# Two transformer blocks on one core: a later slot for the last pair of heads, reordered small work in block 2, and the first input in smaller parts

## The reference

```python
for l in range(DEPTH):                       # block 2
    x = x + 0.5 * swiglu_2(rms_norm_2(x, norm_ffn1[l]), w_gate, w_up, w_down)
    x = x + hybrid_mixer(rms_norm_2(x, norm_mix[l]), w_in[l], ...)
    x = x + 0.5 * swiglu_2(rms_norm_2(x, norm_ffn2[l]), ...)
...
def compress(k, pos, w1, w2):                # keys (CK) and values (CV) of the compressed part
    blocks = k[:, :, cidx, :] + pos
    flat = blocks.reshape(B, G, n_cmp, CMP_LEN * Dh)
    return jax.nn.gelu(flat @ w1) @ w2
kc, vc = compress(k_cmp, ...), compress(v_cmp, ...)
p_c = masked_softmax(einsum(q, kc) * scale, valid_c)
o_cmp = einsum(p_c, vc)
```

## Time and profile before

| what | value |
|---|---|
| median of 3 runs | 2076.1 us (2075.55 to 2076.2) |
| the profiled execution: its time / its span | 2075.85 us / 2074.1 us |
| PE busy | 2048.1 us, 99% |
| POOL busy | 1579.3 us, 76% |
| ACT busy | 1083.4 us, 52% |
| DVE busy | 795.9 us, 38% |
| PE's share of the chain that ended last | 97% |

### The profile page before, as it was taken

One profiled execution on the slowest core, in us unless ns is written; L12 is line 12 of the kernel. 1 busy time (PEld: TensorE's weight loads), 2 busy tenths in 40 slices (PEclk: granted clock), 3 DMA queues, 4 the chain that ended last, 5 costly groups with the idle time before them and its releaser, 6 DMA issues.

```text
span 2074.1 us, 35496 instructions
## 1 busy us (share of the span) xinstructions
PE 2048.1 (99%) x12396; PEld 1769.1 (85%) x12396; DVE 795.9 (38%) x1788; ACT 1083.4 (52%) x1875; POOL 1579.3 (76%) x668
## 2 busy tenths in 40 slices
PE   8999999999999999999999999999999999999998
PEld 7888998888888898888888888788888889878886
DVE  3223744222322374422242237632233225663223
ACT  5445544444544553544454458654455445755443
POOL 7888746888888875688878886478887887546886
PEclk9999999999999999999999999999999999999999
DMA  7555534555555553455555554445555555454553
GB/s 248 191 185 183 183 113 124 191 190 187 179 186 189 176 183 113 132 190 187 190 175 190 182 191 138 166 162 190 187 189 179 185 183 183 139 184 156 186 191 112
DMA packets 100852, 362.33 MB, mean 175 GB/s; under 512 B 11808, under 2 KB 12448, under 8 KB 100640
## 3 DMA queue, kind: packets, MB, share of 16 engines
q1 hardware_dynamic: 100336, 359.97, 52.7%
q10 hardware_dynamic: 432, 1.22, 0.2%
HBM read 360.10 MB, written 1.05 MB: 174 GB/s over the span
## 4 chain that ended last, share of the span: by engine, by line
PE 97%; DVE 1%; ACT 1%; DMA 1%; issue 0%; ACTq 0%; SPq 0%; DVEq 0%; POOLq 0%
PE twin L591 31%; PE twin L595 20%; PE twin L653 9%; PE twin L655 9%; PE twin L654 9%; PE twin L593 5%; PE twin L594 4%; PE twin L710 1%; PE twin L637 1%; PE twin L767 1%; PE twin L638 1%; PE twin L639 1%; PE twin L773 1%; PE twin L784 1%; PE twin L840 0%; PE twin L1102 0%
## 5 line engine op out<-in xcount | busy, mean ns | idle before, releaser
L561 POOL TENSOR_TENSOR wlo<-raw,whi 128x1024 fp32r<-128x1024 f32 x664 | 1579.1, 2407 | 479.2 <-ACT whi L1260 478.9
L1260 ACT CAST whi<-raw 128x1024 fp32r<-128x1024 f32 x664 | 677.3, 1051 | 73.1 <-PE twin L595 35.6
L595 PE MATMUL twin<-turned,wlo 128*128 128x256 f32 x1952 | 549.7, 282 | 0.0
L591 PE MATMUL twin<-turned,whi 128*128 128x512 f32 x1344 | 480.3, 399 | 1.2 <-DVE turned L1640 1.2
L591 PE MATMUL twin<-early,whi 128*128 128x512 f32 x1344 | 480.0, 398 | 0.5
L595 PE MATMUL twin<-early,wlo 128*128 128x256 f32 x1536 | 431.2, 281 | 0.0
L1700 DVE TENSOR_TENSOR twin<-twin,mix 128x512 f32<-128x512 f32 x168 | 117.5, 699 | 758.0 <-ACT mix L1319 758.0
L595 PEld LDWEIGHTS twin<-turned,wlo 128*128 128x128 f32 x1952 | 371.0, 190 | 3.3
L1319 ACT COPY mix<-twin 128x512 f32<-128x512 f32 x168 | 98.5, 586 | 439.0 <-PE twin L595 439.0
L591 PEld LDWEIGHTS twin<-turned,whi 128*128 128x128 f32 x1344 | 253.1, 188 | 63.7 <-issue 1.6
L591 PEld LDWEIGHTS twin<-early,whi 128*128 128x128 f32 x1344 | 252.4, 188 | 64.2 <-issue 2.0
(11 more groups left out here) (285 smaller groups left out, 2092.6 us busy)
## 6 DMA issues: line engine op xcount, KB each, us to landing
raw<-in_w_dram SPq DMA_DIRECT2D x680, 512.0 KB, 3.3
con<-in_con_dram ACTq DMA_DIRECT2D x1, 1113.5 KB, 7.6
x<-in_x_dram SPq DMA_DIRECT2D x2, 512.0 KB, 6.5
out_dram<-xs SPq DMA_DIRECT2D x4, 256.0 KB, 2.8
mix<-in_last_gain_dram SPq DMA_DIRECT2D x1, 512.0 KB, 4.4
par<-in_par_dram SPq DMA_DIRECT2D x2, 208.0 KB, 4.0
par<-in_par_dram SPq DMA_DIRECT2D x2, 154.0 KB, 3.2
con<-in_con_dram ACTq DMA_DIRECT2D x1, 64.0 KB, 4.4
```

The source lines that it names most:

```text
L561: nc.gpsimd.tensor_tensor(wlo[:, place, :], raw[:, place, :], whi[:, place, :].bitcast(F32), ALU.subtract).then_inc(split_done, 1)
L591: pe.matmul(out, hi, both.rearrange("p c n -> p (c n)"), start=start and k == 0, stop=False, skip_group_check=True)
L595: mm = pe.matmul(out[:, 0:SEQ], lo, both[:, 0, :], start=False, stop=stop and k == KD - 1, skip_group_check=True)
L1260: nc.scalar.copy(whi[:, place, :], raw[:, place, :]).then_inc(hi_done, 1)
```

## The change

Four things are changed.

1. Block 2, in both layers: pair 11 is scored at slot 26 and no longer at 25; by the tables its turn moves from slot 27 to 28 and its weighting from 30 to 31. Pair 1's turn stands ahead of pair 3's scores at slot 12. On ACT, `hidden_exp(0)` stands behind slot 31's split and pair 11's exponentials. On DVE, the values' `hidden_kept(1)` stands ahead of the compressed maxima.
2. Start: the left half of x comes in two quarters with a semaphore each, and SyncE waits for slot 0 to land before it issues slot 1. TensorE turns the first quarter when it is there.
3. Start: slot 0's remainder is made by DVE; GpSimd begins with slot 1.
4. End: the two stores of the right half are issued by ACT, those of the left half by SyncE.

```diff
-SCORED = {..., 17: 8, 19: 9, 21: 10, 25: 11}
+SCORED = {..., 17: 8, 19: 9, 21: 10, 26: 11}
@@ SyncE, start
                         if n < 2:
-                            half = slice(n * 512, n * 512 + 512)
-                            sp.dma_start(x[:, :, half], x_d[:, :, half]).then_inc(s_x[n], 16)
+                            for j in range(2 - n):
+                                cols = slice(n * 512 + j * 256, 512 + n * 512 if n else 256 + j * 256)
+                                sp.dma_start(x[:, :, cols], x_d[:, :, cols]).then_inc(s_x[n + 2 * j], 16)
+                        if n == 0:
+                            sp.wait_ge(s_raw[0], 16)
@@ TensorE, x_turned
                 for j, out in zip((2 * half, 2 * half + 1), outs):
+                    if L.deep + w == 0 and j == 1:
+                        pe.wait_ge(s_x[2], 16)
@@ TensorE, block 2's mixer
                     if c in WEIGHED:
                         weighted(WEIGHED[c])
+                    if c in TURNED and TURNED[c] == 1:
+                        pair_turned(1)
                     if c in SCORED:
                         pair_scores(SCORED[c])
-                    if c in TURNED:
-                        p = TURNED[c]
-                        pe.wait_ge(ev("probs_ready"), L.l * PAIRS + (p + 1))
-                        turn_probs(L, p, m2("P", 2304)[:, p % 3 * 768:(p % 3 + 1) * 768])
+                    if c in TURNED and TURNED[c] != 1:
+                        pair_turned(TURNED[c])
@@ ScalarE, block 2's mixer
-                    if c - 1 == HID0_TURNED:
-                        hidden_exp(0)
                     ...                                  # split_hi(c + ahead), sums_kept
                     if c in SCORED:
                         pair_exps(SCORED[c])
+                    if c - 1 == HID0_TURNED:
+                        hidden_exp(0)
@@ VectorE, block 2's mixer
+                    if c == LAST[CV] + 1:
+                        hidden_kept(1)
                     if c - 1 == CMP_BACK:
                         ...                              # the compressed maxima
-                    if c in ENDED and ENDED[c] in (CK, CV):
-                        hidden_kept(int(ENDED[c] == CV))
+                    if c in ENDED and ENDED[c] == CK:
+                        hidden_kept(0)
@@ VectorE, start
+            dve.sem_inc(split_done, RING)
+            dve.wait_ge(hi_done, 1)
+            dve.tensor_tensor(wlo[:, 0, :], raw[:, 0, :], whi[:, 0, :].bitcast(F32), ALU.subtract).then_inc(split_done, 1)
@@ ScalarE, end (SyncE keeps the left half's two stores)
+            for at, T in enumerate(reversed(range(NT))):
+                act.wait_ge(ev("right_ready"), at + 1)
+                nc.scalar.dma_start(out_d[:, T, 512:D], xs[:, T, 512:D]).then_inc(s_out, 16)
```

More of the change, by code:

```diff
@@ L91 @@
 PAIRS = 12
-SCORED = {8: 0, 10: 1, 11: 2, 12: 3, 13: 4, 14: 5, 15: 6, 16: 7, 17: 8, 19: 9, 21: 10, 25: 11}
+SCORED = {8: 0, 10: 1, 11: 2, 12: 3, 13: 4, 14: 5, 15: 6, 16: 7, 17: 8, 19: 9, 21: 10, 26: 11}
 TURNED = {c + (5 if p == 10 else 2): p for c, p in SCORED.items()}
@@ L360, in m2 @@
             return mix[:, M2_[name]:M2_[name] + width]
-        s_x = [sem(f"x_loaded{half}") for half in range(2)]
+        s_x = [sem(f"x_loaded{part}") for part in range(3)]
         s_rest = sem("rest_of_con_loaded")
@@ L543, in _ @@
             for at, T in enumerate(reversed(range(NT))):
-                for half in range(2):
-                    cols = slice(half * 512, half * 512 + 512)
-                    sp.wait_ge(ev(("left_ready", "right_ready")[half]), at + 1)
-                    sp.dma_start(out_d[:, T, cols], xs[:, T, cols]).then_inc(s_out, 16)
+                sp.wait_ge(ev("left_ready"), at + 1)
+                sp.dma_start(out_d[:, T, 0:512], xs[:, T, 0:512]).then_inc(s_out, 16)
             sp.wait_ge(s_out, 2 * NT * 16)
@@ L561, in split_lo @@
                 nc.gpsimd.tensor_tensor(wlo[:, place, :], raw[:, place, :], whi[:, place, :].bitcast(F32), ALU.subtract).then_inc(split_done, 1)
-            pool.sem_inc(split_done, RING)
+            pool.wait_ge(split_done, 1 + RING)
             for L in layers:
                 mixer = MIX2 if L.blk else MIX1
-                with pool.Fori(0, FFN_SLOTS // RING) as i:
+                begun = L.deep == 0
+                if begun:
+                    for n in range(1, RING):
+                        split_lo(L, n)
+                with pool.Fori(0, FFN_SLOTS // RING - begun) as i:
                     for n in range(RING):
-                        split_lo(L, n, i)
+                        split_lo(L, n, i + begun)
                 for n in range(FFN_SLOTS, FFN_SLOTS + mixer):
@@ L1111, in value, with pair_turned @@
                     return vsw[:, c:c + HD]
+                def pair_turned(p):
+                    pe.wait_ge(ev("probs_ready"), L.l * PAIRS + (p + 1))
+                    turn_probs(L, p, m2("P", 2304)[:, p % 3 * 768:(p % 3 + 1) * 768])
                 def weighted(p):
```

## The result

The changed kernel takes 2082.53 us (median of 9 runs, 2080.57 to 2084.73), the kernel before 2075.9 us beside it (9 runs, 2075.06 to 2076.73). The ratio is 1.0032, 95% interval 1.0024 to 1.0040: slower by 6.6 us, where the prediction had 3.7. The profiled execution is the longest of the nine: 2084.73 us, with a span of 2082.9 us, 8.8 us over the span of before.

What follows compares the result with a forecast made beforehand. TensorE, busy for 99% of the span, was taken as the bound. Terms 2.2 + 2.5 - 0.9 - 0.1 = +3.7 us on 2075.85 gave 2079.55, or 2079.8 us against the runs' median; range 2076.2 to 2082.8 us.

Steps and rivals of the forecast that it cites:

- The mixer's chain: Block 2, slots 25 to 32: slot 31's split delays pair 11's exponentials, `compressed_keys` and slot 34's load; +2.2 and +2.5 us.
- Two signs: Waits expected in the changed trace: a short one at pair 11's turn for ScalarE, some 0.7 us at `compressed_values`.
- The forecast of 3.6 us for slot 34's load: Mixer, slots 30 to 32: time from the load's issue until taken up, against 3.9 us before and a 3.3 us median.
- the two layers cost 2.2 + 2.5: Block 2's mixers: `compressed_values` comes 2.2 us later in the first layer, slot 12 included; the second layer loses 2.5 us.
- The rival of late loads: Slot 34's load, which holds the compressed softmax, takes 4.3 to 5.0 us: 2081.2 to 2082.6 us; chance 0.22.
- Slot 12: Pair 1's turn fills TensorE's 0.99 us wait for pair 2's exponentials: -0.36 us a layer (0 to -0.6).
- The start: Kernel's start: x in quarters lets TensorE start 1.1 us earlier; taken as -0.9 us (-1.2 to 0).
- the lower of the prediction's two branches: Start: if the clock's rise stays at its instant, half of the 1.1 us, 0.55 us, is kept.
- the cover of "less than 1 us": Start: slot 1, issued only after slot 0 has landed, has less than 1 us of cover; costed at nothing.
- The end: Kernel's end: four stores on two queues instead of one; -0.1 us (-0.5 to +0.1).
- The kept copy: At `hidden_turned(1)`, first layer: the 1.26 us wait for the values' kept copy goes, but TensorE is later by more.

Runs made afterwards that it cites:

- e5: The changed kernel with three filling matmuls a layer ahead of the keys' product, none ahead of slot 25's chunk: 2079.68 us, ratio 1.0019.
- the second execution: The traced execution of the changed kernel when it was run once more in a later session, with no edit; median there 2082.77 us, ratio 1.0031.
- e11: The kernel before with pair 1's turn ahead of pair 3's scores at slot 12 and nothing else: 2075.08 us, ratio 0.9996.
- e4: The kernel before with the changed start alone (quarters of x, SyncE's wait for slot 0, slot 0's remainder on VectorE): 2075.32 us, ratio 0.9997.
- e8: The kernel before with pair 1's turn first, the values' kept copy earlier and their GELU's first steps ahead of the compressed sums: 2073.30 us, ratio 0.9986.
- e1: The changed kernel with pair 11's scores back at slot 25, all else as changed: 2074.49 us, ratio 0.9992.
- e7: e1 with the first four steps of the values' GELU ahead of the compressed softmax's sums on VectorE: 2072.72 us, ratio 0.9984.
- e9: e7 without SyncE's wait for slot 0 at the start, so slot 1 is issued right behind the quarters: 2073.25 us, ratio 0.9985.
- e10: e7 with ten matmuls of a table of ones on TensorE ahead of its wait for x: 2073.10 us, ratio 0.9985.
- e2: The changed kernel with pair 11's exponentials and the keys' GELU exponential ahead of slot 31's split on ScalarE, scores still at slot 26: 2078.58 us, ratio 1.0012.

## Why the prediction came out as it did

**The mixer's chain: right, to some tenths.** Freed of the clock's fall, the two layers cost +2.0 and +2.4 us (e5), where the prediction had +2.2 and +2.5. In the changed kernel's trace slot 31's split starts at 1333.47 us (1333.7 forecast), `compressed_keys` at 1337.48 (1337.7), slot 25's chunk waits 1.43 us for GpSimd (1.4). The mixer begins 0.36 us earlier there than on the prediction's scale, which leaves both a tenth late. The time of `compressed_keys` itself is a hit, and of the 2 us that TensorE was to stand 1.46 are there and 0.57 at the compression, where the prediction had put some tenths. The links behind show in e5, whose mixer begins 1.07 us early: load of slot 34 issued at 1339.78 + 1.07 = 1340.9 (1340.7 forecast), `compressed_values` at 1350.0 (1350.2). Two signs came out otherwise: pair 11's turn waits for nobody in the changed kernel, and of the 0.7 us forecast at `compressed_values` 0.47 and 0.53 are there, in the second execution 1.25 and none.

The forecast of 3.6 us for slot 34's load lies between e5's 1342.98 - 1339.78 = 3.2 us and the 4.4 and 3.7 us of the changed kernel (4.4 and 3.4 in the second execution). The prediction's estimate of 3.2 us came from a section that times DMAs issued by GpSimd, and these loads are issued by SyncE; e5 has 3.2 us even so. With 3.2 us the two layers would have cost 3.9 us by the prediction's sum; the 4.1 belong to 3.3 us. That wait for the load is real and wasn't tested by itself.

**The step that failed: "the two layers cost 2.2 + 2.5".** It counted TensorE's work behind the waits at the durations of the earlier trace rows. The clock had entered only at the start; that TensorE's own new waits could cost it the clock was in no term and no rival. It withheld 5.1 us of full-speed time in the profiled execution, where the ruler stands 3.3 + 1.5 us over e5, and 3.4 us in the second, where it stands 2.6 + 0.9 over e5. In the median filling the wait brought 3.1 us (2082.77 - 2079.68). The sum without it holds: e5 stands 3.7 us over before (2079.68 - 2076.0), the forecast sum to a tenth, in part by luck, for an interval of 2 us to either side lies around such a difference. Luck too is that the measured 2082.5 us lie inside the stated range, by 0.3 us: its upper part had been given for late loads.

**The rival of late loads** gave 2081.2 to 2082.6 us, near the result, and has a part in it, but not the main one. In the first layer the load did take 4.4 us, in both executions. In the profiled one it was also issued late, at 1342.54 us, for TensorE at 1.2 GHz freed its place late, and only 0.47 us of waiting are left behind it; in the second it makes 1.25 us. In the second layer of the profiled execution it took 3.7 us, as forecast, and the ruler still shows +4.0. And e5, with the same loads to move and the clock kept up, gives 3.1 us back.

**Slot 12.** -0.36 us a layer was forecast; e11 gives -0.3 and -0.6 on the ruler and -1.0 us in the median. Right within what can be told.

**The start.** -0.9 us was forecast; e4's -0.75 and e8's distance of 0.6 us with the end in it agree, none of them resolved from zero. In the changed kernel's profiled execution x came 0.64 us earlier, not 1.1, and pair 2's scores stand only 0.36 us before their old time. One execution misleads here: over all traces TensorE's first work on x stands at 7.25 to 7.84 us with the old start (four traces) and at 5.86 to 6.61 with the changed one (eight), 1.4 us apart in the median. So x came earlier than forecast, and only about half of that shows in the times, the lower of the prediction's two branches. The new wait of 0.23 us for slot 1's remainder is the cover of "less than 1 us" that was given at nothing; the second execution doesn't have it.

**The end.** -0.1 forecast, -0.1 in the trace.

**The kept copy.** The prediction said that its 1.26 us go and are outweighed. In e1, where nothing outweighs them, they brought little either: on the ruler e1 stands 0.2 to 0.6 us under e11, and 0.61 us of waiting had moved to `compressed_values`. With the further edit of e7 the second layer gains 0.8 us; in the first, 0.74 us are back at `hidden_turned(1)` (1.11 in e9, 0.81 in e10).

**What isn't settled.** Why the first layer of one execution loses 3.4 us to the clock, and its other layer and both of the second execution 1.7. How the changed kernel's 3.1 us over e5 divide between the clock and slot 34's load, which took 4.4 us in both first layers and 3.2 in e5's. And what each wait of e2 would give back if it were filled alone.

## What to carry to other kernels

Where TensorE bounds a kernel, price a new wait at its length and look at what TensorE does right before and after it: a run of small matmuls with two waits of 0.6 and 1.5 us in it cost some 3 us beyond the waits, most of it through the clock, and six idle matmuls in the longer wait (three a layer) bought them back. Runs whose times follow their mean granted clock (4 us from 0.999 to 0.996) are the sign, visible without a trace. A wait that is taken away in a chain of three engines tends to come up again one link on, so follow the queue of each engine one step past the wait before the gain is booked.

## What the runs showed of the hardware

- The clock fell from 2.4 to 1.2 GHz in the middle of a kernel whose TensorE is busy for 99% of the span. Ahead of the fall lay waits of 0.57 and 1.46 us in 2.7 us, with only eight small matmuls (0.64 us in all, 32 columns of weights each) between them. The kernel before has a wait of 1.26 us in the same chain, and 1.00 throughout.
- The fall outlasts the waits: TensorE had been busy without a gap from 1337.48 us, and was still at 0.50 through 1342 us. In e10 the clock, raised early, fell at the end of a wait of 1.48 us.
- Of 5.1 us that the clock withheld in the profiled execution, 4.8 (ruler, against e5) reached the end of the layers, and for 3.4 us in the second execution 3.5; slot 34's load has a part in both, of 0.47 and 1.25 us of waiting in the first layer.
- One and the same kind of load, slot 34's 512 KB, took 3.2 to 4.4 us from issue to ScalarE's split (six layers of three traces), with the longest in both first layers in which the clock had fallen.
